# Wide matmuls on the high half of the first expert table, with the half sums added on GpSimd

## The reference, cut to what matters

```python
q = (h @ w_q)                     # 1024 -> 2048: 8 heads x 2 halves x 128
s = einsum(q, sub_keys)           # 128 scores for each half of each head
... top 16 of each half, then the 16 best of the 256 sums, softmax -> gates g, indices idx
act = gelu(einsum('thkd,td->thk', u_tab[idx], h))
out = einsum('thk,thkd->td', g * act, v_tab[idx])
```

## Time and profile before

| what | value |
|---|---|
| median of 3 runs | 2659.87 us (2658.42 to 2661.96) |
| span of the profiled execution, first to last instruction | 2658.5 us |
| what lies around the span, against that median | 1.4 us |
| TensorE matmul busy | 2445.7 us, 92% |
| VectorE busy | 1683.0 us, 63% |
| ScalarE busy | 1293.7 us, 49% |
| GpSimd busy | 0.4 us |
| mean granted TensorE clock | 0.973 |

### The profile page before, as it was taken

One profiled execution on the slowest core, in us unless ns is written; L12 is line 12 of the kernel. 1 busy time (PEld: TensorE's weight loads), 2 busy tenths in 40 slices (PEclk: granted clock), 3 DMA queues, 4 the chain that ended last, 5 costly groups with the idle time before them and its releaser, 6 DMA issues.

```text
span 2658.5 us, 51578 instructions
## 1 busy us (share of the span) xinstructions
PE 2445.7 (92%) x17556; PEld 2270.0 (85%) x17556; DVE 1683.0 (63%) x3490; ACT 1293.7 (49%) x2816; POOL 0.4 (0%) x5
## 2 busy tenths in 40 slices
PE   7999979999985799999799999889999985899998
PEld 2767879999985799999677777789999985899998
DVE  2565247888769766665225674238888769766665
ACT  1456145555568655554123422055555568555554
POOL 0000000000000000000000000000000000000000
PEclk9989989999999999999899899999999999999999
DMA  6345444555530355555232212445555530355554
GB/s 229 136 168 189 150 143 163 183 183 181 184 119 0 103 182 182 183 183 178 98 127 88 80 56 80 135 142 183 181 181 182 183 103 0 121 182 183 183 184 143
DMA packets 108502, 388.94 MB, mean 146 GB/s; under 512 B 12784, under 2 KB 15088, under 8 KB 107776
## 3 DMA queue, kind: packets, MB, share of 16 engines
q1 hardware_dynamic: 104256, 380.16, 42.5%
q10 hardware_dynamic: 4160, 7.61, 0.9%
HBM read 386.67 MB, written 1.05 MB: 146 GB/s over the span
## 4 chain that ended last, share of the span: by engine, by line
PE 84%; DVE 9%; issue 3%; ACT 2%; DVEq 0%; ACTq 0%; DMA 0%; PEld 0%; PEldq 0%
PE ps L1308 20%; PE ps L1310 20%; PE ps L1309 20%; PE ps L707 19%; DVE arena L1574 2%; DVE gbuf L1540 2%; PE ps L789 2%; PE ps L1000 1%; PE ps L978 1%; PE ps L1565 1%; PE ps L1340 1%; DVE gbuf L801 0%; PE ps L992 0%; PE ps L1236 0%; ACT arena L772 0%
## 5 line engine op out<-in xcount | busy, mean ns | idle before, releaser
L1308 PE MATMUL ps<-hsplit,hl 128*128 128x256 f32 x2304 | 655.9, 285 | 31.7 <-DVE hl L1380 31.7
L1309 PE MATMUL ps<-hsplit,hl 128*128 128x256 f32 x2304 | 655.0, 284 | 0.0
L1310 PE MATMUL ps<-hsplit,hl 128*128 128x256 f32 x2304 | 654.9, 284 | 0.0
L1308 PE MATMUL ps<-csplit,hl 128*128 128x256 f32 x2048 | 581.1, 284 | 6.2 <-DVE hl L1606 6.2
L1309 PE MATMUL ps<-csplit,hl 128*128 128x256 f32 x2048 | 581.0, 284 | 0.0
L1310 PE MATMUL ps<-csplit,hl 128*128 128x256 f32 x2048 | 581.0, 284 | 0.0
L1377 ACT CAST hl<-ring 128x512 fp32r<-128x512 f32 x576 | 355.6, 620 | 387.2 <-PE ps L1310 386.8
L1380 DVE TENSOR_TENSOR hl<-ring,hl 128x512 fp32r<-128x512 f32 x576 | 397.6, 692 | 221.2 <-ACT hl L1377 187.4
L1308 PEld LDWEIGHTS ps<-hsplit,hl 128*128 128x128 f32 x2304 | 445.7, 193 | 32.8 <-ACT hl L1377 32.8
L707 PE MATMUL ps<-arena,ring 128*128 128x256 f32 (+2 forms) x1896 | 447.6, 395 | 15.5 <-issue 10.8
L1309 PEld LDWEIGHTS ps<-hsplit,hl 128*128 128x128 f32 x2304 | 445.7, 193 | 0.0
(11 more groups left out here) (196 smaller groups left out, 2019.7 us busy)
## 6 DMA issues: line engine op xcount, KB each, us to landing
ring<-stream SPq DMA_DIRECT2D x723, 512.0 KB, 3.3
arena<-keys ACTq DMA_DIRECT2D x2, 1024.0 KB, 4.9
gbuf<-consts ACTq DMA_DIRECT2D x1, 1120.0 KB, 5.1
arena<-xT ACTq DMA_DIRECT2D x1, 1024.0 KB, 10.4
arena<-ctxT ACTq DMA_DIRECT2D x1, 1024.0 KB, 12.7
resid<-xT ACTq DMA_DIRECT2D x1, 1024.0 KB, 8.9
out<-resid SPq DMA_DIRECT2D x1, 1024.0 KB, 3.9
gbuf<-consts ACTq DMA_DIRECT2D x1, 832.0 KB, 6.3
```

Of the source, the lines that this page charges most:

```text
L1308: pe.matmul(out_ap, w[0], m[0], start=start, stop=False)
L1309: pe.matmul(out_ap, w[1], m[0], start=False, stop=False)
L1310: return pe.matmul(out_ap, w[0], m[1], start=False, stop=stop)
```

## The change

`passes` stays for table `v`. For `wq` and `u` a new function makes two matmuls for each k-tile: high weights by both parts of the tokens (512 columns, the whole bank), and low weights by the high tokens (256 columns, added to the first half of the bank). The bank then holds two partial sums that have to be added. ScalarE copies all 512 columns into a new buffer of two places, GpSimd adds the two halves into `acts` or `q_area` and counts `u_summed`. ScalarE applies Gelu in place to four units at a time, one group behind. `take_unit` now also waits until GpSimd has read the place that it writes. The scores wait for the sums of `wq`, and the hots for all Gelus.

```diff
+    halves_buf, _ = place("halves_buf", [P, 2, 2, T])
...
+    def wide_passes(pe, bank, w_hi, w_lo, m_both, start, stop):
+
+        pe.matmul(ps[:, bank, :], w_hi, m_both, start=start, stop=False)
+        return pe.matmul(ps[:, bank, 0:T], w_lo, m_both[:, 0, :], start=False, stop=stop)
+
     UB = 4
     N_IT = P // UB
+    SUM_RING = 2
...
+    def sums_before(b, table):
+
+        return (b - 1) * (NQ + P) + BEFORE[table]
...
         pe.wait_ge(S("u_bank_free"), banks_freed(b, "u") + 4)
+        pe.wait_ge(S("u_summed"), sums_before(b, "u"))
...
-                    m = [hsplit[:, x, k, :] for x in range(2)]
-                    mm = passes(eng, ps[:, s % 4, 0:T], w, m, k == 0, k == KD - 1)
+                    mm = wide_passes(eng, s % 4, w[0], w[1], hsplit[:, :, k, :], k == 0, k == KD - 1)
...
             take_unit(eng, b, i, s - 2, per, table)
+            if table == "u" and s % 4 == 3 and not first:
+                gelu_units(eng, b, i, s - 7, per)
+
+    def gelu_units(eng, b, i, s, per=4):
+
+        eng.wait_ge(S("u_summed"), i * per + (sums_before(b, "u") + s + 4))
+        four = acts[:, ds(i * (per * T) + s * T, 4 * T)]
+        eng.activation(four, four, ACT.Gelu).then_inc(S("u_gelu"), 1)
...
         eng.wait_ge(S("split_used"), i * 2 * per + (halves(b, table) + HLRING * b + 2 * s + 2))
-        dst, func = (acts, ACT.Gelu) if table == "u" else (q_area, ACT.Copy)
-        eng.activation(dst[:, ds(i * (per * T) + s * T, T)], ps[:, s % 4, 0:T], func).then_inc(S("u_bank_free"), 1)
+        done = sums_before(b, table) + s + 1 - SUM_RING
+        if not (b == 1 and table == "wq") or not isinstance(i, int) or i * per + done > 0:
+            eng.wait_ge(S("u_summed"), i * per + done)
+        eng.copy(halves_buf[:, s % SUM_RING, :, :], ps[:, s % 4, :].rearrange("p (h t) -> p h t", h=2))\
+           .then_inc(S("u_bank_free"), 1)
+
+    def pool_sum(pool, b, i, s, table):
+
+        pool.wait_ge(S("u_bank_free"), i * 4 + (banks_freed(b, table) + s + 5))
+        dst = acts if table == "u" else q_area
+        pool.tensor_tensor(dst[:, ds(i * (4 * T) + s * T, T)], halves_buf[:, s % SUM_RING, 0, :],
+                           halves_buf[:, s % SUM_RING, 1, :], ALU.add).then_inc(S("u_summed"), 1)
...
         pe.wait_ge(S("u_bank_free"), banks_freed(b + 1, "wq"))
+        pe.wait_ge(S("u_gelu"), b * N_IT)
...
         take_unit(act, b, N_IT, -1)
+        gelu_units(act, b, N_IT, -4)
...
             pool.memset(ones, 1.0).then_inc(S("ones_ready"), 1)
+            for b in (1, 2):
+                for table, n in (("wq", NQ // 4), ("u", N_IT)):
+                    with pool.Fori(0, n) as i:
+                        for s in range(4):
+                            pool_sum(pool, b, i, s, table)
```

## The result

The changed kernel takes 2679.1 us (median of 4 runs), the kernel before 2659.6: 1.0069 of the time, 95% interval 1.0057 to 1.0082. It is slower by about 19 us, and the forecast was 16 us faster. The time lies near the second rival's 2684.

What follows compares the result with a forecast made beforehand. TensorE bounds, VectorE close behind; a layer saves 6.9 us in free units and 8.0 in top-k, loses 4.1 in lookups and 2.8 at the ends: 8.0 us, 16 in two layers, giving 2644 us; range 2614 to 2690.

Steps and rivals of the forecast that it cites:

- the second rival: Top-k stretch: GpSimd's add makes VectorE the bound; at 0.35 us a unit the kernel takes 2684 us, slower; chance 0.27.
- What bounds the kernel: u part: TensorE sets the pace at 2.87 us a unit; VectorE's own chain is 2.67 in top-k units, slack 0.20.
- Part 3: GpSimd's 288 adds, 0.69 us each, off TensorE's path; in top-k units each lengthens VectorE's chain by 0.10 us.
- turning point: Top-k stretch: the add's cost to VectorE, 0.20 us a unit, from which on the kernel is slower than before.
- Part 3, the lookups: 24 lookup units a layer: the add costs VectorE 0.46 us a unit on average, making 3.02; they lose 4.1 us.
- Part 1: Matmuls of wq and u: one weight load fewer for each k-tile saves 21.5 ns, 0.172 us a unit.
- The third rival: Wide matmul of wq and u: it saves nothing because fp32r columns are slow by themselves; 2674 us; chance 0.13.
- the 40 free units: 16 of wq, 8 of the gate part, 16 at the end of a layer: VectorE half busy; save 6.9 us.
- Part 2: ScalarE: copy of 512 columns 0.59 us, Gelu of 1024 columns 1.06; 2.09 us in a unit of 2.70, costing nothing.
- Part 4: Ends of wq and u, where TensorE waits for copy, add and Gelu: 2.8 us more a layer, from 1.9 to 3.5.

## Why the prediction was wrong, point by point

**What bounds the kernel.** Right in the order: TensorE at 2.88 us a unit, and VectorE close behind it in the top-k stretch. (I counted 569 matmuls in 68 us, two of them cut by the window's edges; from start to start it is 120.0 ns, so 360 ns for a k-tile.) The slack was too large. I took the 15.7 us of waits in the earlier trace rows for slack, 0.20 us a unit, and VectorE's own chain for 2.67. But a wait that the profile names takes in the short pause that stands ahead of a subtraction anyway. The run with the wide matmul alone, where VectorE hardly waits in layer 2, shows its chain as 2.77 us; against the 229.2 us before, the slack was 7.7 us or 0.10 a unit.

**Part 3, the step that failed: "I put 0.10 us a unit on the add: VectorE's chain 2.77, just above TensorE's 2.70".** Measured, the top-k unit went to 240 / 80 = 3.00 us, 0.33 over my 2.67. Of that 0.10 is the chain itself, which is 2.77 without any add, and 0.23 is the add. VectorE's busy time says the same, 194.5 to 213.0 us in layer 1, which is 0.23 a unit:

```profile
404.22:633.41 229.19, 228.35 (x1892) 228.38 (x1893) 194.42 (x624) 121.04 (x238) 0.00 (x0) 0.99 0.54 181
```

```profile
402.90:643.85 240.95, 238.69 (x1273) 195.58 (x1274) 213.03 (x624) 154.08 (x259) 62.09 (x79) 0.99 0.52 172
```

(Before and after, columns as in the earlier trace rows.) With the chain at 2.77, even the add of the forecast, 0.10, would have given 2.87 and no gain in the top-k stretch. The mechanism was the one named (an add keeps a subtraction out); the way of sizing it was wrong. I compared a mean gap of 0.7 us with an add of 0.69, as if the add began where the gap begins. It begins when ScalarE's copy ends, wherever VectorE is then, and even tied to the gap it needs 0.26 us to begin and 0.75 to run. This was the second rival, with its turning point at 0.20 and 2684 us at 0.35. That its time came so near owes something to luck: 0.35 was half an add on a chain of 2.67, and two terms together made 0.33. The add's own length was fairly sized: 0.75 us undisturbed, where I took 0.69 and the ratio of the Trainium skill (GPSIMD Engine Reference, Performance versus the Vector engine) gave an estimate of 0.82; 0.86 with its waits. The Trainium skill's rule (SBUF — State Buffer, SBUF: two separate sides) agrees with these traces: subtractions went from 693 to 798 ns on average and singly to 1.30 us, while index searches and maxima kept their time. I had put 0.27 on this case; so small a slack against an add of more than three times that should have made it the forecast.

**Part 3, the lookups.** The 3.02 us a unit were too much; 25 units took 70.0 us, 2.80 a unit. I charged VectorE 0.46 us a unit for the add; its busy time grew by 0.21. Where VectorE's two-input operations follow closely on each other, GpSimd mostly waits (adds of 1217 ns, 0.47 us over the wq stage's).

**Part 1.** The term of 21.5 ns a k-tile was too large: 6.7 in the changed kernel's last units (360.0 to 353.3), 8.7 on average in the run with the wide matmul alone. I took the 217.7 ns for 512 columns from plain float32 matmuls, and 512 fp32r columns take 232 to 237. The third rival was nearly right in its mechanism. This term alone would have shrunk the gain: the 40 free units of a layer save about 2 us and not 6.9. It didn't set the sign. VectorE's 3.0 us a unit would cover any saving of TensorE in the top-k stretch.

**Part 2.** Right: copy 0.58, Gelu 1.06, and ScalarE's part alone costs nothing where it stands.

**Part 4.** 3.5 us a layer where I had 2.8; the rest are the times from one engine to the next.

Left open: why the k-tiles stand at 347 ns in some stretches and at 353 in others, with the same instructions. Whether a GpSimd instruction that reads nothing from SBUF collides too was not tried.

## What to carry to other kernels

Before work goes to GpSimd, find VectorE's real slack in that stretch: its waits for data, by unit, less the pause that stands ahead of such an operation where it doesn't wait. Set it against the whole length of the GpSimd instruction, not against what sticks out over a mean gap. In these runs the loss stayed below that length: the add of 0.75 us cost 0.23 a unit of the top-k stretch in VectorE's busy time, two of them 0.41, the copy of 0.40 up to 0.05. If both must share a stretch, cut GpSimd's work until a piece with its start fits into nearly every gap between VectorE's two-input operations, and let each piece wait for the operation ahead of its gap; here the cut alone brought 11 us, the wait 3, both 31. A weight load that is hidden behind streaming is worth only the few ns that show between matmuls: read them from a stream of the same data type.

## What the runs showed of the hardware that was not expected

- A matmul of 512 fp32r columns takes 232 to 237 ns at full clock, nearly twice the 120.0 of 256 columns in the kernel before, with the columns in one piece of memory or in two. Two loads in place of three save 6.7 to 13.3 ns a k-tile.
- A GpSimd add of 128x256 float32 takes 0.75 us where VectorE leaves it alone, one of 128x128 0.46, a copy of 128x256 0.40.
- VectorE's float32 copy of 128x256 within SBUF has one input and is lengthened by GpSimd all the same, from 285 ns in the kernel before to 422 on average. The 8 of 32 that begin while an add runs take 0.84 us, the other 24 0.28 to 0.29. From the groups of the changed kernel:

```profile
L1439 DVE COPY keybuf<-s_area 128x256 f32 x32 | 13.5, 422 | 0.0
```

- With the sums alone, the same instructions took 231.3 us in one layer's top-k stretch and 241.7 in the other's.
